# Rotary embedding without the matmul exchange, and a later wait for the shifted residual, in a three-layer fp32 forward pass

## The reference, cut to what matters

```python
def apply_partial_rope(t, cos, sin):          # ROT_DIM = 16 of 64 dimensions
    x1, x2, rest = tf[..., :half], tf[..., half:ROT_DIM], tf[..., ROT_DIM:]
    out = jnp.concatenate([x1 * c - x2 * s, x2 * c + x1 * s, rest], axis=-1)
...
    q = apply_partial_rope(q.reshape(B, S, N_Q_HEADS, HEAD_DIM), cos, sin)
    k = apply_partial_rope(k.reshape(B, S, N_KV_HEADS, HEAD_DIM), cos, sin)
...
    x = layer_norm(ALPHA * x + mix, ln1_g, ln1_b)
    up = causal_dwconv_2(jnp.einsum('bsd,df->bsf', x, w_up), ffn_conv_w)
    a, b = jnp.split(up, 2, axis=-1)
    ffn = jnp.einsum('bsf,fd->bsd', jax.nn.silu(a) * b, w_down)
    return layer_norm(ALPHA * x + ffn, ln2_g, ln2_b)
```

## Time and profile before

| | |
|---|---|
| median of 3 runs | 1207.84 us (1206.76 to 1208.05) |
| the profiled execution, its own time | 1206.72 us |
| its span in the trace | 1204.9 us, mean granted clock 0.998 |
| busy: TensorE, VectorE, ScalarE, GpSimd | 1187.3, 844.7, 713.6, 428.0 us |
| read from HBM | 210.31 MB, 175 GB/s over the span |

### The profile page before, as it was taken

One profiled execution on the slowest core, in us unless ns is written; L12 is line 12 of the kernel. 1 busy time (PEld: TensorE's weight loads), 2 busy tenths in 40 slices (PEclk: granted clock), 3 DMA queues, 4 the chain that ended last, 5 costly groups with the idle time before them and its releaser, 6 DMA issues.

```text
span 1204.9 us, 27024 instructions
## 1 busy us (share of the span) xinstructions
PE 1187.3 (99%) x10148; PEld 1165.6 (97%) x10148; DVE 844.7 (70%) x1389; ACT 713.6 (59%) x1242; POOL 428.0 (36%) x405
## 2 busy tenths in 40 slices
PE   8999999999999999999999999999999999999997
PEld 7999999999999999999999999999999999999997
DVE  5868665676877765767667877756767677877754
ACT  5767667545766654466456666545466456666543
POOL 3007315123343402222339444424412349444422
PEclk9999999999999999999999999999999999999999
DMA  7655455554666666454654666565545554666563
GB/s 259 184 165 160 127 158 170 189 187 157 194 193 192 190 191 192 157 160 142 188 179 142 208 191 192 176 201 167 158 158 158 184 177 150 204 195 192 178 196 100
DMA packets 60286, 212.68 MB, mean 177 GB/s; under 512 B 6688, under 2 KB 7968, under 8 KB 60064
## 3 DMA queue, kind: packets, MB, share of 16 engines
q1 hardware_dynamic: 60192, 211.39, 56.8%
HBM read 210.31 MB, written 1.05 MB: 175 GB/s over the span
## 4 chain that ended last, share of the span: by engine, by line
PE 92%; DVE 4%; POOL 1%; ACT 1%; issue 1%; POOLq 0%; DVEq 0%; ACTq 0%
PE bank L1091 29%; PE bank L1093 28%; PE bank L1092 28%; PE bank L1107 1%; DVE wlo L1397 1%; PE bank L1215 1%; PE bank L1246 1%; PE bank L1226 1%; PE bank L1270 1%; POOL u L673 0%; PE bank L1202 0%; ACT whi L756 0%; DVE prob L1537 0%; DVE u L1629 0%; DVE prob L1562 0%
## 5 line engine op out<-in xcount | busy, mean ns | idle before, releaser
L1397 DVE TENSOR_TENSOR wlo<-raw,whi 128x1024 fp32r<-128x1024 f32 (+1 forms) x400 | 497.4, 1245 | 212.0 <-ACT whi L756 205.8
L1091 PE MATMUL bank<-shifted,whi 128*128 128x256 f32 x2296 | 639.0, 278 | 1.5 <-POOL shifted L692 1.1
L1092 PE MATMUL bank<-shifted,whi 128*128 128x256 f32 x2296 | 636.2, 277 | 0.0
L1093 PE MATMUL bank<-shifted,wlo 128*128 128x256 f32 x2296 | 635.9, 277 | 0.0
L756 ACT ACTIVATE whi<-raw 128x1024 fp32r<-128x1024 f32 (+1 forms) x400 | 416.6, 1042 | 153.2 <-PE bank L1093 134.7
L1091 PEld LDWEIGHTS bank<-shifted,whi 128*128 128x128 f32 x2296 | 431.6, 188 | 3.3 <-POOL shifted L692 1.3
L1093 PEld LDWEIGHTS bank<-shifted,wlo 128*128 128x128 f32 x2296 | 431.8, 188 | 0.0
L1092 PEld LDWEIGHTS bank<-shifted,whi 128*128 128x128 f32 x2296 | 431.2, 188 | 0.0
L652 POOL TENSOR_TENSOR fprod<-ugate,uval 128x256 f32<-128x256 f32 x66 | 94.1, 1426 | 197.7 <-DVE uval L1712 188.4
L1091 PE MATMUL bank<-fhi,whi 128*128 128x256 f32 x528 | 145.9, 276 | 0.0
L1093 PE MATMUL bank<-fhi,wlo 128*128 128x256 f32 x528 | 145.9, 276 | 0.0
(11 more groups left out here) (218 smaller groups left out, 1253.9 us busy)
## 6 DMA issues: line engine op xcount, KB each, us to landing
raw<-in_w_win SPq DMA_DIRECT2D x140, 512.0 KB, 3.6
raw<-in_w_up SPq DMA_DIRECT2D x132, 512.0 KB, 3.6
raw<-in_w_down SPq DMA_DIRECT2D x48, 448.0 KB, 3.5
raw<-in_w_merge SPq DMA_DIRECT2D x32, 512.0 KB, 3.6
raw<-in_w_out SPq DMA_DIRECT2D x24, 512.0 KB, 3.6
raw<-in_w_down SPq DMA_DIRECT2D x24, 512.0 KB, 3.5
x<-in_x SPq DMA_DIRECT2D x4, 256.0 KB, 4.0
rgw<-in_rg_w SPq DMA_DIRECT2D x1, 1024.0 KB, 10.5
```

The lines of the kernel that those rows point to most:

```text
L1091: pe.matmul(ps, whi[:, slot, w], hi, start=first, stop=False)
L1092: pe.matmul(ps, whi[:, slot, w], lo, start=False, stop=False)
L1093: return pe.matmul(ps, wlo[:, slot, w], hi, start=False, stop=last)
L1397: dve.tensor_tensor(wlo[:, n % RING, w], raw[:, n % RING, w], whi[:, n % RING, w].bitcast(f32), ALU.subtract) \
```

## The change

It has two parts. The first: in the later layers the exchange of the paired rows is made by VectorE with a shuffle of the partitions inside each group of 32 (`stream_shuffle` with the list `EXCHANGE`, which swaps rows 0 to 7 with 8 to 15 and leaves the others), and TensorE's matmul and the constant `swap` are gone. The sign moves into the column `freq`, whose first eight rows are negated, so that their sines are too. The cosine product goes to GpSimd as a step of its own, into `tmp[:, 2, :]`; it waits for the copy of the tile and for the rotary step before. VectorE adds the two products after a wait for GpSimd's. The second: VectorE's wait for all shifts of x moves from ahead of the down phase to ahead of its first residual, behind the low parts of the third, fourth and fifth units, and GpSimd makes the last low part of the activations ahead of the last shift. In `wout` the wait moves to the same place before the first residual.

```diff
-CONST = {"ident": 0, "swap": P, "alibi": 2 * P, "slide": 5 * P, "count": 8 * P, "freq": 8 * P + 2 * S}
+CONST = {"ident": 0, "alibi": P, "slide": 4 * P, "count": 7 * P, "freq": 7 * P + 2 * S}
...
-            c[head + half + i, CONST["swap"] + head + i] = -1.0
-            c[head + i, CONST["swap"] + head + half + i] = 1.0
             f = np.float32(500000.0) ** (-np.float32(2 * i) / np.float32(16))
-            for j in (i, half + i):
-                c[head + j, CONST["freq"]] = f
+            c[head + i, CONST["freq"]] = -f
+            c[head + half + i, CONST["freq"]] = f
...
+EXCHANGE = [i + 8 if i < 8 else i - 8 if i < 16 else i for i in range(32)]
...
-                if step[0] in ("turn_v", "turn_v2", "rg_gates", "rope", "pool_mix"):
+                if step[0] in ("turn_v", "turn_v2", "rg_gates", "pool_mix"):
...
 (GpSimd)
+            def step_rope(l, i):
+                tile = K2 if i == 0 else Q2 + i - 1
+                pool.wait_ge(copied, copies_before(l) + tile + 1)
+                wait(pool, roped, 5 * l + i)
+                if l == 0 and i == 0:
+                    pool.wait_ge(prep, 3)
+                pool.tensor_tensor(tmp[:, 2, :], u2[:, tile, :], rope_cs[:, 0, :], ALU.mult).then_inc(rope_cos, 1)
...
                 repeat(pool, name, UPT, 6, body, peel_first=True)
+                low(FT - 1)
                 if which is not None:
                     shift_x(which, KT - 1)
-                low(FT - 1)
...
 (TensorE)
-            def step_rope(l, i):
-                u = MISC[("rope", l, i)]
-                tile = K2 if i == 0 else Q2 + i - 1
-                pe.wait_ge(copied, copies_before(l) + tile + 1)
-                wait(pe, misc_read, u)
-                pe.matmul(ps_misc[:, 0:S], swap, u2[:, tile, :], start=True, stop=True).then_inc(misc_done, 1)
...
 (VectorE)
             def step_rope(l, i):
-                dve.wait_ge(misc_done, MISC[("rope", l, i)] + 1)
-                t = u2[:, K2 if i == 0 else Q2 + i - 1, :]
-
+                tile = K2 if i == 0 else Q2 + i - 1
+                t = u2[:, tile, :]
+                dve.wait_ge(copied, copies_before(l) + tile + 1)
                 wait(dve, roped, 5 * l + i)
-                dve.tensor_tensor(tmp[:, 3, :], ps_misc[:, 0:S], rope_cs[:, 1, :], ALU.mult).then_inc(misc_read, 1)
-                link(dve.tensor_tensor(t, t, rope_cs[:, 0, :], ALU.mult))
-                dve.wait_ge(misc_read, MISC[("rope", l, i)] + 1)
-                dve.tensor_tensor(t, t, tmp[:, 3, :], ALU.add).then_inc(roped, 1)
+                link(dve.stream_shuffle(tmp[:, 3, :], t, EXCHANGE))
+                link(dve.tensor_tensor(tmp[:, 3, :], tmp[:, 3, :], rope_cs[:, 1, :], ALU.mult))
+                dve.wait_ge(rope_cos, 5 * l + i + 1)
+                dve.tensor_tensor(t, tmp[:, 2, :], tmp[:, 3, :], ALU.add).then_inc(roped, 1)
...
             def wout(name, which, alpha, begun=0):
-                if which in LNI:
-                    dve.wait_ge(x_shifted, KT * (LNI[which] + 1))
                 for t in range(KT):
                     if t >= begun:
                         lo_part(START[name] + t + 2)
+                    if t == 0 and which in LNI:
+                        dve.wait_ge(x_shifted, KT * (LNI[which] + 1))
                     residual(name, t, START[name] + t, alpha, bank_of(RESULT[name] + t), which)
...
             def down(name, which, alpha):
-                if which in LNI:
-                    dve.wait_ge(x_shifted, KT * (LNI[which] + 1))
-
                 def body(n, i, it):
                     lo_part(n + 2, it, 6)
...
                     t = i // 3
+                    if i == 2 and isinstance(it, int) and which in LNI:
+                        dve.wait_ge(x_shifted, KT * (LNI[which] + 1))
                     if i % 3 == 2:
                         residual(name, t, n, alpha, down_bank(name, t), which, it, 6, 2)
```

More of the change, by code:

```diff
@@ L293, in cst @@
             return const[:, CONST[name]:CONST[name] + n]
-        ident, swap = cst("ident", P), cst("swap", P)
+        ident = cst("ident", P)
         bank = [ctx.enter_context(nc.psum_tensor(f"bank{i}", [P, 512], f32)) for i in range(8)]
@@ L337, in build @@
         angles, sines, roped, lam_exp, prep = sem("angles"), sem("sines"), sem("roped"), sem("lam_exp"), sem("prep")
+        rope_cos = sem("rope_cos")
         pooled, pool_y, pool_hi, pool_lo = sem("pooled"), sem("pool_y"), sem("pool_hi"), sem("pool_lo")
@@ L627, in step_rg_hidden @@
                 pool.tensor_tensor(u1[:, XR + t, :], u1[:, ROOT + t, :], u1[:, RGATE + t, :], ALU.mult).then_inc(rg_hidden, 1)
-            STEPS = {"table": step_table, "pool_sums": step_pool_sums, "rg_input": step_rg_input, "rg_hidden": step_rg_hidden,
+            STEPS = {"rope": step_rope, "table": step_table, "pool_sums": step_pool_sums, "rg_input": step_rg_input, "rg_hidden": step_rg_hidden,
                      "diff_diag": step_diff_diag, "shift_x": step_shift_x}
@@ L1281, in step_pool_mix @@
                 mm.then_inc(misc_done, 1)
-            STEPS = {"turn_v": step_turn_v, "turn_v2": step_turn_v2, "rope": step_rope, "scores": step_scores,
+            STEPS = {"turn_v": step_turn_v, "turn_v2": step_turn_v2, "scores": step_scores,
                      "weights": step_weights, "values": step_values, "diff_sums": step_diff_sums, "diff_spread": step_diff_spread,
```

## The result

The changed kernel took 1200.8 us (median of 5 runs, 1200.48 to 1203.1) against 1208.05 us before: ratio 0.9949, 95% interval 0.9938 to 0.9959, so 5.0 to 7.5 us faster. The forecast was 1202.1 us, in a range from 1200.0 to 1205.2.

The account below looks back on a forecast made before the run. The prediction took TensorE to bound the kernel, busy 99% of the span. Its terms, -4.9 + 0.6 - 1.36 = -5.7 us, taken from the median 1207.84, gave 1202.1 us, in a range from 1200.0 to 1205.2.

Parts of the forecast that it names:

- the sign: Whole kernel: faster by over 0.2% (below 1205.4 us) 0.87, within 0.2% 0.10, slower 0.03.
- the likeliest case: Whole kernel: the forecast's own case, 1200.2 to 1204.0 us, chance 0.66.
- The exchange: Later layers' rotary steps: removing TensorE's ten exchange matmuls saves 4.9 us, between 4.4 and 6.2.
- VectorE keeps up: Later layers' rotary steps: shuffle 0.35 us, step about 1.25; with low part 2.4 us of a 2.72 us unit.
- GpSimd's products: Later layers' rotary steps: ten more GpSimd cosine products of 0.7 to 1.5 us, done before VectorE's sum needs them.
- The loss at the first weights: Before each later layer's first turned weights: VectorE late, gap of 0 to 0.7 us, taken as 0.6 for both.
- The residual's wait: Third down unit, both later layers: TensorE's gap of 0.68 us each goes, -1.36 us, between 0.8 and 1.4.
- Sum: Whole kernel: -4.9 + 0.6 - 1.36 = -5.7 us.
- Rival A: Rotary steps: every new product and low part slowed beside GpSimd, gap 1.2 to 1.7 us a layer; 1204.5 us; chance 0.18.
- B: Scores and weights around 540 to 560 us: TensorE's saved time given back, only residual's gain left; 1206.5 us; chance 0.10.
- C: Later layers' rotary steps: shuffle has a large fixed cost, 1.2 us or more; at 1.3 us, 1211 us; chance 0.03.

Follow-up runs that it names:

- sums_after_weights: Kernel after, with GpSimd's pool sums held until VectorE has scaled the second head's weights: 1200.73 us, ratio 0.9929.
- wait_alone: Kernel before, with only VectorE's wait for the shifts moved, GpSimd's order old: 1207.47 us, one execution.
- order_alone: Kernel before, with only GpSimd's last low part of the activations put ahead of the last shift: 1206.75 us, one execution.
- shuffles_four: Kernel after, with each shuffle made four times over, same result: 1210.64 us, ratio 1.0025.
- sums_late: Kernel after, with GpSimd's pool sums waiting until 14 input tiles are copied instead of 8: 1201.02 us, ratio 0.9952.
- sums_in_two: Kernel after, pool sums held until the second head's weights are scaled, those behind the three doublings until the fourth head's: 1203.59 us, ratio 0.9954.
- rotary_only: Kernel after, with the down phase's wait for the shifted residual and GpSimd's order put back as before: 1204.35 us, ratio 0.9972.

## Why the prediction was right

The time, the sign and the likeliest case came true. That the sum is met within 0.2 us is luck: by the stages the loss at the weights was 1.05 us larger than taken, and the two gains together 0.94 us larger. The steps:

- **The exchange**, -4.9 us. sums_after_weights has the exchange removed and no gap in its place: 2.50 and 2.79 us below the kernels with the exchange, -5.3 us. The kernels with the exchange have no gap at any weights either, so the new place of the sums adds nothing to this. The chain's share was short by 0.4 us. Counted from start to start, from the last matmul before an exchange to the fifth behind it, the ten in the trace of the kernel before cost 0.46 to 0.62 us each beyond five steps, 5.15 us together: the first matmuls behind each step more slowly, and neither the share of L1202 nor the reading to the second matmul counts all of that.
- **VectorE keeps up.** Right. The shuffle is 0.44 instead of 0.35 us, within its bounds; the step takes 1.35 us. With the sums out of the way (sums_after_weights) VectorE waits 1.00 us for the first scores. No idle time of VectorE for the cosine product shows, in layer 1 neither.
- **GpSimd's products**, 0.7 to 1.5 us: 0.73 to 1.70.
- **The loss at the first weights**, 0.6 us: mis-sized, and for another reason than the one given. Measured: 5.29-3.64 = 1.65 us for both layers. I had VectorE come late out of its last rotary step, 0.8 to 1.9 us earlier than before. It came to the scores 2.21 us earlier, outside that range, and the low part at 515.94 started 2.49 us earlier, with TensorE 2.6 us early. By my working this leaves no gap at all. It arose behind: 0.26 us in that low part, 0.55 us in the sum of two columns and 0.91 us in the scaling. With the 0.12 us that were missing at the low part's start these make 1.84 us, less 1.0 us of slack 0.84 us. The step that failed was the reading of the earlier trace rows. I took the pool sums to end at about 511.5, but that row holds only their first three additions; the whole job ran to 518.8, close ahead of the scaling. So I priced what the sums lay over before, and not what they would lie over. This was also the term in which I took a value near the mild end without a row for it.
- **The residual's wait**, -1.36 us: right as the price of the gap, too small for the stage. The gap of 0.68 us went in both layers, as worked out, and its halves (wait_alone, order_alone) behave by the same working, but the stages are 0.95 us shorter, -1.9 us. The 0.27 us more lie around the third to fifth units, where the kernel before steps at 0.1176 us for some 7 us. The gap does not by itself bring these slow steps (last section), so this part of the gain came unforeseen and stays unexplained.
- **Sum.** -5.3+1.65-1.9 = -5.5 us from the stages, against -5.7 forecast, and -6.2 (-7.5 to -5.0) from the runs. The prediction's case held. Rival A asked for 1.2 to 1.7 us of gap a layer, a figure that does not follow from the terms listed with it; 0.8 was measured. B is refuted by the stages, C did not occur, and shuffles_four shows what it would have cost.

## What to carry to other kernels

When one engine is sped up, list what of the others lay just beside its needs: a long, uncritical job on GpSimd that overlapped nothing important before may now overlap the VectorE step that has no slack. Look up where such a job ends, and not only where its first row ends. Hold such a job by a semaphore to the stretch where VectorE is idle anyway, and check both ends of it, since here too late (sums_late, sums_in_two) cost as much as too early. Compare stages of the trace rather than medians where a kernel's start varies more than the change is worth.

## What the runs showed of the hardware

**A scalar product on VectorE is slowed by GpSimd too.** The scaling of weights has one tensor operand and went from 0.55 to 1.46 us for two, both times with GpSimd at work (kernel after, sums_late), and stayed at 0.55 for the same heads in sums_after_weights. Over the thirteen traces, the 334 single scalings in the later layers without a GpSimd operation beside them took 285 to 291 ns (128x128) or 340 to 353 ns (128x256); beside one they took up to 1194 and 901 ns, in the kernel before too, at the shifts of x. In the kernel after the delay lasts just as long as GpSimd's operation: the sum of two columns ends 0.02 us and the first scaling 0.08 us after the GpSimd operation beside it. The Trainium skill, SBUF — State Buffer, "Who interferes with whom", names `tensor_scalar` among the operations that can take the port pair shared with GpSimd; this agrees. The prediction's wording of that section's rule, that an instruction with a single SBUF input does not contend, left this exception out. The shuffle, also with one input, kept 435 to 451 ns in the kernel after, next to GpSimd (at 507.16) or not.

**Matmuls can step more slowly with the same granted clock.** In the kernel before the steps from 780 to 786 us are 0.1176 us, then 0.1133 us, at a granted clock of 1.00. I first took this for an effect of the gap ahead of it. The gap alone does not bring it: rotary_only has the same gap in both layers (0.79 and 0.80 us) and the slow steps only in layer 0, order_alone has a longer gap (0.97 us) and steps at 0.113 to 0.116 us right behind it, and sums_after_weights steps at 0.1177 us from 655.6 to 662.6 us with no gap ahead. What causes it stays open; a stretch of 7 us costs about 0.3 us.

**The start varies by a drop of the clock.** The stage up to the first out-projection took 290.9 to 291.5 us in the five traces with a granted clock of 1.00 from 16 to 24 us, and 293.0 to 294.2 us in the eight with 0.57 to 0.79. Windows 8 to 16 and 16 to 24 us (busy us of each engine, granted clock, DMA share, GB/s) of the kernel after and of sums_late:

```profile
8.00:16.00 8.00, 6.04 (x44) 5.31 (x42) 5.41 (x12) 4.58 (x11) 1.23 (x3) 1.00 1.03 418
16.00:24.00 8.00, 6.79 (x57) 6.38 (x56) 4.99 (x8) 4.02 (x8) 5.50 (x4) 1.00 0.69 223
```

```profile
8.00:16.00 8.00, 5.76 (x40) 4.97 (x39) 4.57 (x10) 4.44 (x9) 0.86 (x2) 1.00 1.02 414
16.00:24.00 8.00, 6.88 (x33) 6.25 (x32) 5.12 (x9) 2.58 (x6) 5.57 (x4) 0.58 0.60 217
```

In the second, TensorE is granted a mean of 0.58 for 8 us, which lies between its two levels, 1.2 and 2.4 GHz (0.5 and 1), and gets through 33 matmuls instead of 57. It had been busy for 5.76 us of the 8 us before, against 6.04, but that does not tell the two apart: rotary_only was busy for 6.15 us there and was granted 0.79. These 2 to 3 us are up to half of what the whole change brings, and lie 460 us ahead of it.
